# Layer embedding and Hyena filters in one block: sine layers beside gate products, norms by token columns, the next projection's first half begun there

## The reference

```python
    # end of the first block
    pg = jax.nn.sigmoid(rmsnorm(x, norm_ple[i]) @ w_ple_gate[i])
    x = x + pg * (p[i] @ w_ple[i])
    return rmsnorm(x, norm_final)

    # start of the second block
    h = _rmsnorm(x, norm_mix_g[i])
    y = _hyena_mixer(h, ...)          # z = conv(h @ w_in + b_in) is its first step

def _hyena_filter(L, w1, b1, w2, b2, w3, b3, w4, freq):
    ...
    hdn = jnp.sin(fq * (z @ w1.astype(f32) + b1.astype(f32)))
    hdn = jnp.sin(fq * (hdn @ w2.astype(f32) + b2.astype(f32)))
    hdn = jnp.sin(fq * (hdn @ w3.astype(f32) + b3.astype(f32)))
    k = hdn @ w4.astype(f32)
    ...
    k = k * jnp.exp(-t * jnp.tile(deltas, 2)[None, :])
```

## Time and profile before

| | us |
|---|---|
| median of 3 runs | 4157.64 |
| lowest and highest run | 4155.96, 4166.61 |
| span of the profiled execution | 4162.8 |
| PE busy in it | 3890.4 |
| mean granted TensorE clock | 0.962 |

### The profile page before, as it was taken

One profiled execution on the slowest core, in us unless ns is written; L12 is line 12 of the kernel. 1 busy time (PEld: TensorE's weight loads), 2 busy tenths in 40 slices (PEclk: granted clock), 3 DMA queues, 4 the chain that ended last, 5 costly groups with the idle time before them and its releaser, 6 DMA issues. The chain is left out here.

```text
span 4162.8 us, 63294 instructions
## 1 busy us (share of the span) xinstructions
PE 3890.4 (93%) x26374; PEld 3063.9 (74%) x26374; DVE 2293.3 (55%) x3312; ACT 1324.7 (32%) x2130; POOL 1332.2 (32%) x537
## 2 busy tenths in 40 slices
PE   8999999988989999978787999999999999999998
PEld 6855788865767887567675788877777877887886
DVE  5746477456667765558785677375550526242024
ACT  3245233233214332434444333232222111103222
POOL 1001444422314441000001344365554342663442
PEclk9999999999999999989998999999999999999998
DMA  5310222222212222341111122221212121322221
GB/s 172 122 61 22 101 81 100 105 103 81 81 41 101 101 101 102 143 169 59 44 44 65 63 101 101 101 77 72 81 61 86 56 77 53 120 96 86 83 99 61
DMA packets 43488, 361.46 MB, mean 87 GB/s; under 512 B 4355, under 2 KB 4739, under 8 KB 23916
## 3 DMA queue, kind: packets, MB, share of 16 engines
q1 hardware_dynamic: 43244, 357.95, 23.8%
HBM read 334.34 MB, written 23.07 MB: 86 GB/s over the span
## 5 line engine op out<-in xcount | busy, mean ns | idle before, releaser
L346 POOL TENSOR_TENSOR ffn_weights_low<-weight_ring,ffn_weights_high 128x2048 fp32r<-128x2048 f32 x128 | 591.2, 4619 | 789.9 <-ACT ffn_weights_high L443 789.2
L202 PE MATMUL banks<-ffn_in_high,ffn_weights_low 128*128 128x512 f32 x2048 | 803.8, 392 | 18.5 <-POOL ffn_weights_low L357 7.2
L203 PE MATMUL banks<-ffn_in_low,ffn_weights_high 128*128 128x512 f32 x2048 | 800.9, 391 | 0.0
L204 PE MATMUL banks<-ffn_in_high,ffn_weights_high 128*128 128x512 f32 x2048 | 800.8, 391 | 0.0
L202 PEld LDWEIGHTS banks<-ffn_in_high,ffn_weights_low 128*128 128x128 f32 x2048 | 387.2, 189 | 103.6 <-POOL ffn_weights_low L357 11.6
L204 PEld LDWEIGHTS banks<-ffn_in_high,ffn_weights_high 128*128 128x128 f32 x2048 | 386.9, 189 | 81.2
L203 PEld LDWEIGHTS banks<-ffn_in_low,ffn_weights_high 128*128 128x128 f32 x2048 | 387.3, 189 | 80.5 <-issue 0.7
L443 ACT ACTIVATE ffn_weights_high<-weight_ring 128x2048 fp32r<-128x2048 f32 x128 | 245.2, 1915 | 562.0 <-PE banks L204 562.0
L3597 POOL TENSOR_TENSOR third_weights_low<-weight_ring,third_weights_high 128x1024 fp32r<-128x1024 f32 x144 | 364.3, 2530 | 11.6
L590 DVE SCALAR_TENSOR_TENSOR ffn_gate<-ffn_up,columns_sb,ffn_gate 128x511 f32<-128x511 f32 (+1 forms) x132 | 273.5, 2072 | 160.8 <-ACT ffn_value L486 160.8
L3595 POOL CAST third_weights_high<-weight_ring 128x1024 fp32r<-128x1024 f32 x144 | 158.8, 1103 | 520.5 <-PE banks L204 484.5
(11 more groups left out here) (609 smaller groups left out, 7386.6 us busy)
## 6 DMA issues: line engine op xcount, KB each, us to landing
weight_ring<-weights SPq DMA_DIRECT2D x144, 2048.0 KB, 7.7
scan_in<-rwkv_operands SPq DMA_DIRECT2D x7, 1280.0 KB, 6.6
rwkv_operands<-rwin_staged SPq DMA_DIRECT2D x24, 256.0 KB, 2.3
scan_in<-rwkv_operands SPq DMA_DIRECT2D x8, 512.0 KB, 4.0
bias_tiles<-bias_rows SPq DMA_DIRECT2D x8, 448.0 KB, 8.9
residual<-x SPq DMA_DIRECT2D x4, 512.0 KB, 7.0
filt_decay<-decay SPq DMA_DIRECT2D x1, 2048.0 KB, 8.2
rwkv_residual<-residual SPq DMA_DIRECT2D x1, 2048.0 KB, 7.1
```

Source lines behind the costliest of these rows:

```text
L202: pe.matmul(out, w[1], x[0], start=start, stop=False, skip_group_check=True)
L203: pe.matmul(out, w[0], x[1], start=False, stop=False, skip_group_check=True)
L204: return pe.matmul(out, w[0], x[0], start=False, stop=stop, skip_group_check=True)
L346: pool.tensor_tensor(parts[1], landed, parts[0].bitcast(F32), ALU.subtract).then_inc(S["split"], 1)
```

## The change

`layer_embedding` and `hyena_filters` become one stage, `embedding_and_filters`, with 60 semaphores and one barrier instead of two.

- The small filter table (positions and the three layers) and the decay table are loaded at the start of the stage, beside pT, into buffers of their own.
- The three layer matmuls stand between the gate tiles: after the fifth of eight k steps of the first tile pair, after tile 3, and after tile 5. DVE's chain for each and ACT's sine stand between their gate work.
- The squares of the new x are taken by ACT tile by tile as the residual adds finish, and added by POOL (six adds). For the second norm POOL adds three and DVE three.
- Both norms' sums are taken by token columns: four blocks of 128 tokens as stationary operand against one column of ones, so that mean, root and reciprocal work on a 128x4 tile (`G.roots`). `root_spread` brings it back to 128x512 in a bank, and ACT copies it.
- The joins of spectra 1 to 3 come after the split of h.
- The first half of the next stage's first chunk is split in pieces in this stage, the second half as a whole, and PE does the first two projection tiles here (banks 4 and 5). `hyena_projection` starts with its third tile; its bank order is turned (4 * (1 - p)).
- Buffers are laid out so that the next stage's weight parts live beside this stage's.

The core of the diff:

```diff
+            def layer(n):
+                rows = EMB if n == 0 else FILTER
+                if n == 0:
+                    pe.wait_ge(S["small_loaded"], 16)
+                else:
+                    pe.wait_ge(S["sine_done"], n)
+                pe.matmul(G.banks[:, LAYER_BANK[n], :], small[0:rows, SEQ + n * P:SEQ + (n + 1) * P],
+                          small[0:EMB, 0:SEQ] if n == 0 else arg[0:FILTER, 2, :], start=True, stop=True).then_inc(S["layer_sum"], 1)
...
+                if k == KT // 2:
+                    layer(0)
+            for m in range(2, KT):
+                pe.wait_ge(S["split"], m // 2 + 1)
+                if m == 6:
+                    pe.wait_ge(S["bank_read"], 2)
+                if m == 7:
+                    pe.wait_ge(S["bank_read"], 3)
...
+                if m == 3:
+                    pe.wait_ge(S["square_added"], KT - 1)
+                    pe.matmul(G.banks[:, 7, :], G.con("ones"), square_sum, start=True, stop=True).then_inc(S["summed"], 1)
+                    layer(1)
+                if m == 5:
+                    pe.wait_ge(S["mean_done"], 1)
+                    layer(2)
...
+            def sums(parts, bank, done):
+                for j in range(JT):
+                    for n, of in enumerate(parts):
+                        mm = pe.matmul(G.banks[:, bank, j:j + 1], of[:, j * P:(j + 1) * P], G.con("ones")[:, 0:1],
+                                       start=(n == 0), stop=(n == len(parts) - 1))
+                mm.then_inc(done, 1)
+
+            for n in range(3):
                 taps(n)
+            pe.wait_ge(S["x_added"], KT - 2)
+            pe.wait_ge(S["x_squared"], KT)
+            pe.wait_ge(S["gated"], KT)
+            sums((squares[:, 0, :], squares[:, KT - 1, :]), X_BANK, S["x_sums"])
+            for n in range(3, 5):
                 taps(n)
+            pe.wait_ge(S["x_inverse"], 1)
+            root_spread(pe, G, X_BANK, S["x_spread"])
+            taps(5)
+            G.arrived(pe, TABLE_CHUNK, 0)
+            pe.wait_ge(S["tapped"], 8)
+            spectrum(0, (S["x_rstd"], 1))
+            taps(6)
+            pe.wait_ge(S["tapped"], 2 * 6)
+            pe.wait_ge(S["h_low_added"], KT // 2 - 1)
+            pe.wait_ge(S["h_high_added"], KT // 2 - 1)
+            sums((squares[:, 0, :], squares[:, KT // 2, :]), H_BANK, S["h_sums"])
+            pe.wait_ge(S["h_mean"], 1)
+            taps(7)
+            pe.wait_ge(S["tapped"], 2 * len(ROUNDS))
+            pe.wait_ge(S["h_inverse"], 1)
+            root_spread(pe, G, H_BANK, S["h_spread"])
+            spectrum(1, (S["h_rstd"], 1))
+            for n in range(2, 4):
                 spectrum(n)
+            pe.wait_ge(S["joined"], 6)
+            for k in range(KT):
+                pe.wait_ge(S["next_piece_split"], k + 1)
+                pe.wait_ge(S["h_split"], k + 1)
+                for m in range(2):
+                    mm = exact_product(pe, G.banks[:, 4 + m, :], [w[:, k, m * P:(m + 1) * P] for w in next_half(0)[1]],
+                                       [x[:, k, :] for x in T.h_parts], start=(k == 0), stop=(k == KT - 1))
...
@@ hyena_projection
         @block.gpsimd
         def _(pool):
-            landed, parts = landed_half(0)
-            for k in range(KT):
-                pool.wait_ge(S["piece_high"], k + 1)
-                pool.tensor_tensor(parts[1][:, k, :], landed[:, k, :], parts[0][:, k, :].bitcast(F32), ALU.subtract).then_inc(S["piece_split"], 1)
-            pool.wait_ge(S["piece_split"], KT)
-            pool.sem_inc(S["split"], 1)
-            for n in range(1, halves):
+            pool.sem_inc(S["split"], 2)
+            for n in range(2, halves):
...
-            for k in range(KT):
-                pe.wait_ge(S["piece_split"], k + 1)
-                for m in range(2):
-                    mm = product(0, m, k)
-                    if k == KT - 1:
-                        mm.then_inc(S["tile_sum"], 1)
+            pe.sem_inc(S["tile_sum"], 2)
```

POOL's and DVE's new adds, and DVE's order from the residual adds on:

```diff
+            for k in range(1, KT - 1):
+                pool.wait_ge(S["x_squared"], k + 1)
+                if k > 1:
+                    pool.wait_ge(S["x_added"], k - 1)
+                pool.tensor_tensor(squares[:, 0, :], squares[:, 0, :], squares[:, k, :], ALU.add).then_inc(S["x_added"], 1)
+            for k in range(1, KT // 2):
+                pool.wait_ge(S["h_squared"], k + 1)
...
+            for n in range(3):
+                taps(n)
+            mean(X_BANK, S["x_sums"], S["x_mean"])
+            taps(3)
+            invert(S["x_root"], S["x_inverse"])
+            for n in range(4, 6):
+                taps(n)
+            dve.wait_ge(S["x_rstd"], 1)
+            for k in range(KT):
                 dve.scalar_tensor_tensor(out=G.x[:, k, :], in0=G.x[:, k, :], scalar=G.col("norm_final", k), in1=rstd[:, :],
                                          op0=ALU.mult, op1=ALU.mult).then_inc(S["x_normed"], 1)
+            for k in range(KT // 2 + 1, KT):
+                dve.wait_ge(S["h_squared"], k + 1)
...
+            taps(6)
+            mean(H_BANK, S["h_sums"], S["h_mean"])
+            invert(S["h_root"], S["h_inverse"])
+            taps(7)
             join(0)
```

More of the change, by code:

```diff
@@ new lines, in embedding_and_filters @@
+        even = G.sb("ple_even", [P, 2, 2, HALF_D], ctx=ctx)
+        pT, p_parts, small, w_parts, sg, arg, rstd = T.pT, T.p_parts, T.small, T.ple_parts, T.sg, T.arg, T.rstd
+        decay = lambda j, of: T.u_x0[:, 1, (1 - of) * JT + j, :]
+        x_parts = T.h_parts
+        sq, square_sum = sg, G.hT[:, 0, :]
+        squares = G.hT
+        both = lambda of, s, j: T.u_x0[:, of, s * JT + j, :]
+        ROUNDS = [(of, j) for of in range(2) for j in range(JT)]
+        SPECTRA = [(of, q) for of in range(2) for q in range(2)]
@@ new lines, in _ @@
+            for k in range(KT):
+                act.activation(sq[:, k, :], G.x[:, k, :], ACT.Square).then_inc(S["squared"], 1)
+            act.wait_ge(S["p_loaded"], 16)
+            for k in range(2):
+                act.activation(p_parts[0][:, k, :], pT[:, k, :], ACT.Copy).then_inc(S["p_high"], 1)
+            act.wait_ge(S["gate_sum"], 2)
+            high(2)
+            sine(0)
+            act.wait_ge(S["gate_sum"], 4)
+            high(3)
+            rms_root(act, G, S, rstd)
+            sine(1)
@@ new lines, in _ @@
+            sine_in(0)
+            for k in range(1, KT):
+                dve.wait_ge(S["squared"], k + 1)
+                if k > 1:
+                    dve.wait_ge(S["square_added"], k - 1)
+                dve.tensor_tensor(square_sum, sq[:, 0, :] if k == 1 else square_sum, sq[:, k, :], ALU.add).then_inc(S["square_added"], 1)
+            for k in range(2):
+                dve.wait_ge(S["p_high"], k + 1)
+                dve.tensor_tensor(p_parts[1][:, k, :], pT[:, k, :], p_parts[0][:, k, :].bitcast(F32), ALU.subtract).then_inc(S["p_split"], 1)
@@ L1906, in _ @@
             h_split(KT - 1)
-            join(3)
-        G.first += 2
+            for n in range(1, 4):
+                join(n)
+        G.first += 5
 def hyena_projection(G, T):
@@ L1917, in hyena_projection @@
     with ExitStack() as ctx:
-        S = stage(G, "hyin", ctx, "edges", "tile_sum", "biased", "centre", "left", "right", "product", "piece_high", "piece_split", "rounded", "split")
+        S = stage(G, "hyin", ctx, "edges", "tile_sum", "biased", "centre", "left", "right", "product", "rounded", "split")
         z = G.sb("hyin_z", [P, 4, SEQ + 2], ctx=ctx)
         c = T.x0T[:, 4:8, :]
-        w_parts = [G.sb("hyin_weights_" + part, [P, 2, CHUNK // 2], F32R, ctx=ctx) for part in ("high", "low")]
+        w_parts = T.w_parts
         h_parts = T.h_parts
```

439 lines of the change are left out of this document (199 added, 240 removed).

## The result

| | before | changed kernel |
|---|---|---|
| median of the runs shown together, us | 4157.57 (4 runs) | 4130.32 (4 runs, 4125.8 to 4132.0) |
| ratio to before, 95% interval | | 0.9928, 0.9915 to 0.9941 |
| span of the profiled execution, us | 4162.8 | 4127.1 |
| PE busy in it, us | 3890.4 | 3883.8 |
| mean granted TensorE clock | 0.962 | 0.962 |

The ratio is that of the means; the medians give 0.9934. The sign and most of the mechanism came out; the size didn't.

The account below looks back on a forecast made before the run. TensorE, busy 93% of the span, bounds the kernel; only its idle or low-clock time can be won. The stretch's terms sum to 80.6 us against 96.3 before, gain 15.7, so 4141.9 us; range 4135 to 4152.

Parts of the forecast that it names:

- gate stretch: Gate tiles on PE: three layer matmuls move in between them, +2.6 us, nothing else late.
- three waits: PE waits: 2.3 us after two tap rounds, 3.4 before the second norm's sums, 0.9 before round 7's products pass DVE.
- low clock behind the waits: PE at low clock after the first two waits: 3.0 us chosen, from nothing to 6.8 possible.
- product of the next tiles: 48 projection matmuls at 0.233 us right behind spectrum 3: 11.2 us.
- boundary: Start of the projection: PE's third tile waits 0.3 us for the barrier and 4.3 for POOL's 60 semaphore clears.
- restart: After the boundary PE restarts at low clock: 6.13 us for 14 matmuls instead of 3.17, so 3.0.
- Sine chains hidden: Three DVE/ACT chains among the gate tiles, each held once by POOL up to 4.5 us, covered; 21.0 us before first tap go.
- rival of chains that don't hide: Sine chains held twice by POOL, plus three low-clock restarts: 4.1 us slower, 4162; chance 0.05.
- Products and squares by turns: DVE's residual adds beside POOL's square adds alternate at about 1.8 us; DVE ends at 915.0 and PE waits 2.3.
- Second norm: After tap round 5, DVE's scalings and adds beside POOL make PE wait 3.4 us, then another 0.9 before round 7's products.
- Sums of token columns: Each norm's sums are 16 PE records, 2.1 us, and a spread 1.1; two norms 6.4.
- rings run freer: Rival: neither DVE–POOL–ACT wait drops the clock, or the first vanishes; gain 21.7 us, 4136; chance 0.14.

Follow-up runs that it names:

- two edits: Changed kernel with ScalarE instead of POOL handing the split half-chunks to PE: 4121.64 us; changed kernel with semaphores cleared by ranges of numbers: 4114.79 us.
- the ranges alone: Changed kernel with each stage's semaphores cleared by ranges of neighbouring numbers, 22 clears instead of 534: 4114.79 us, ratio 0.9884.
- the last kernel: Changed kernel with semaphores cleared by ranges and the h squares given to PE in four parts: 4111.5 us, ratio 0.988.
- the padding: Kernel before with unused bytes ahead of the projection's weight parts: 32 bytes 4154.23 us; 512, 128 and 256 bytes 4149.96, 4158.24 and 4152.24 us.

## Why the prediction missed its size

From the first gate matmul to the last of the projection, by the terms of my sum (us):

| term | forecast | measured |
|---|---|---|
| gate stretch, longer by | 2.6 | 3.8 |
| eight tap rounds | 14.1 | 14.2 |
| spectra | 28.1 | 27.3 |
| sums and spreads | 6.4 | 5.3 |
| three waits | 6.6 | 4.6 |
| handoffs | 1.0 | 0.8 |
| low clock behind the waits | 3.0 | 3.5 |
| product of the next tiles | 11.2 | 11.3 |
| boundary | 4.6 | 4.8 |
| restart | 3.0 | 2.6 |
| pitch of 528 more projection matmuls | no term | -3.5 |

The gate stretch aside, up to the third tile I had 75.2 and it is 72.05. 3.2 less there, 0.4 at the restart, 3.5 by the pitch, and 1.2 given back in the gate stretch: 5.9 over the 15.7, which is the 21.5 measured within rounding. Behind the stretch lie 2.5 more (2.5 + 1.0 - 1.0); the 3.3 that remain of the 27.3 are within what two medians of four such runs tell, and the profiles place no more than about 5 behind the stretch in all. So, by the prediction's steps:

- **First tap within 0.5 of the last embedding matmul: right**, 0.23.
- **Gate stretch +2.6: too small.** A layer matmul costs more than its two records. PE rows:

```profile
884.26 0.39 PE L204 MATMUL banks<-hyena_normed_high,ple_weights_high 128*128 128x512 f32 x1
884.58 1.12 PE L1672 MATMUL banks<-filt_arg,filter_layers 64*128 64x512 f32 x2
885.63 0.50 PE L202 MATMUL banks<-hyena_normed_high,ple_weights_low 128*128 128x512 f32 x1
```

  From 884.26 to 885.63 it is 1.37 where two matmuls of a three-pass product would be 0.23 apart, and the next is late by another 0.1: 1.25 each, three times.
- **Sine chains hidden: right, and two of the three holds by POOL too.** Chain 1 ran free. Chains 2 and 3 were held in their second step, the first that has no input from PSUM, by POOL's halves of 873.66 and 886.68 (4.61 each):

```profile
857.32 0.47 DVE L1873 TENSOR_SCALAR filt_arg<-filt_arg 128x512 f32<-128x512 f32 x1
...
874.43 4.12 DVE L1873 TENSOR_SCALAR filt_arg<-filt_arg 128x512 f32<-128x512 f32 x1
...
888.66 2.92 DVE L1873 TENSOR_SCALAR filt_arg<-filt_arg 128x512 f32<-128x512 f32 x1
```

  No PE wait among the gate tiles came of it. The rival of chains that don't hide is refuted.
- **Products and squares by turns: right in kind, too dear.** I gave the shared residual adds 1.3 and a period of 1.8, from one row of a subtraction:

```profile
904.69 1.07 DVE L1913 TENSOR_TENSOR residual<-residual,ple_gate 128x512 f32<-128x512 f32 x1
905.69 0.68 DVE L1911 TENSOR_TENSOR ple_gate<-ple_gate,banks 128x512 f32<-128x512 f32 x1
906.40 1.07 DVE L1913 TENSOR_TENSOR residual<-residual,ple_gate 128x512 f32<-128x512 f32 x1
```

  They take 1.07 with a period of 1.71. DVE began these products 1.2 late, with the gate stretch, and was at its first tap at 910.77 all the same, which is 914.9 on before's axis where I had 915.0. PE came to its third round 1.2 later than planned as well, and so waited 0.96 and not 2.3. The Trainium skill (SBUF — State Buffer, "Who interferes with whom") has the pair of ports held for a whole instruction by whoever issues first. The trace agrees: DVE's 4.12 above ends 0.28 behind POOL's instruction, and without POOL's adds DVE's residual adds took 0.69, not 1.07.
- **Second norm: 3.4 forecast, 2.84 measured; 0.9 forecast, 0.78 measured.** Right.
- **Low clock: 3.0 forecast behind both waits, 3.5 measured, all behind the second.** Behind 0.96 none came.
- **Sums of token columns 2.1 each: too dear.** 16 records cost PE 1.70, a spread 0.9 to 1.0, not 1.1. The row of eight records that I doubled stands at its start behind a wait; in a full queue the start is hidden.
- **Table loads 1.28 with no drain: right.** ACT's rows:

```profile
862.73 1.28 ACT L1788 ACT_TABLE_LOAD   x1
864.03 0.63 ACT L1788 ACTIVATE filt_arg<-filt_arg 128x512 f32<-128x512 f32 x1
```

  The sine starts 1.30 behind the load. The Trainium skill (ScalarE: Activation LUTs, "What ACT_TABLE_LOAD costs") gives some 2.66 per switch; the measurement decides.
- **Boundary 4.6, restart 3.0: right**, 4.8 and 2.6, and shown by two edits to be POOL's clears. In the changed kernel's trace the 60 clears start 0.071 apart, from 974.95 to 979.13.
- **The failed step** is in the prediction's first sentence and in where its sum ends. It said that "only PE's idle time, and work that PE does at a low clock, can be won", but PE's rate at full clock could be won too. "48 matmuls at 0.233 (the pitch of that stage at full clock)" took the pitch for the stage's own. The change re-lays the buffers, as its last item says, and the 528 matmuls behind the third tile, for which the sum had no term, went from 0.2333 to 0.2267: 3.5 us. With that the forecast would have been 4138.4. The small terms, most of them too dear, bring it to 4136.1, which is the stretch as measured.

That would still lie in the range. What carried the result out of it is a second term put at nothing: I took the stretch off the median as if all behind it stayed. The medians have 5.8 us there. 2.5 of them are the RWKV projection's, for which no view of before gave a reason and whose cause stays open; the other 3.3 are not told from chance.

The range left all this out on one side only: its lower end, 4135, was made of the rings' terms alone. The rival "rings run freer" came nearest (4136), and for a part of its reasons: the first wait dropped no clock.

## What to carry to other kernels

When a change moves buffers, compare the pitch of the same matmul from stage to stage first: a rate that differs where no wait is shown was here a cost of placement, and a re-layout can take or give it. Count what POOL does between two stages: semaphores cleared one by one are 0.07 us each in front of its first work, and whoever waits for that work pays for it, here up to 16 us of the program. Judge a part worth 3 us on a stretch of the timeline, not on medians whose executions differ by 10 to 20, and only after the length of the low clock in both stretches has been compared: here it made up to 3 us by chance.

## What was not expected of the hardware

- The start-to-start time of an fp32r matmul of 512 columns (the type of the high and low parts) was 0.2333 or 0.2267 us by where its weight parts lay in SBUF (the table above), with PE's clock granted in full in both.
- A wait isn't always followed by a low clock, and not by the same length of it. Behind the stage's start, with 4.4 us of idle PE each time, the low level lasted 6.8 us in the changed kernel and 3.4 in two of its variants and in one of before; behind 3.0 it was none in one kernel (the ranges alone) and 3.4 in another (with the four parts). Behind the same 2.84 at the second norm it was 6.8 in the changed kernel, and 3.4, 10.2 and 13.7 in three variants. Behind the 0.96 in the changed kernel none came, behind the 1.36 of the last kernel one of 3.4.
- One SP issue of a transfer near the end of the RWKV projection took 1.4 to 2.5 us in one kernel's eight profiles and at most 0.66 in the other's nine. Neither two transfers more nor the padding took it away.
